# A transformer layer with expert look-up on one core: row norm taken out of the queries, head 0's queries first, queries made turned, scores read in PSUM

## The chip, the cores and the metric

One core of a Trainium2 chip. The time is device microseconds from start to end of one execution of the whole layer.

## The reference, cut to what matters

```
h = rms_norm(x, norm1_g);  x = x + mixer(h) @ w_out          # the front: products and attention
h = rms_norm(x, norm2_g)                                     # 256 rows of 2048
q = h @ w_query                                              # 2048 x 2048, 8 heads of 2 x 128
s = q . sub_keys                                             # per head two rows of 128 scores
top 16 of each, top 16 of the 256 sums -> expert_idx, g = softmax(best)
u, v = expert_u[expert_idx], expert_v[expert_idx]            # rows of 2048 floats
act = gelu(u . h);   x = x + sum (g * act) v
```

A row of h is x times a gain, times one factor for the row (rstd). This factor is a positive number common to all scores of a row, so the choice of the top 16 does not depend on it.

## The kernel before, in words

All 256 rows are two tiles (t) of 128 partitions. Products of fp32 are made of two halves: a weight step of 1024 columns (0.5 MB) is loaded by SP into one of four raw buffers, ACT copies it into `split_hi` (`hi_steps`, L450), DVE takes the difference into `split_lo` (`lo`, L653), and PE makes three products for each pair (`gemm_step`, L1165 to L1167). There are two split buffers, so step n needs the space of step n - 2; SP loads step n when lo n - 4 is done.

The front ends with the out-projection, 4 chunks of 512 columns with 8 steps each. After each chunk DVE adds it to x (`to_x1`, L967) and squares it. Then for the query product: the row norm is made (POOL takes the power, L375), ACT and DVE scale a tile of rows each (L475, L672), PE turns the rows (L1152), ACT and DVE split them into `ht` (L464, L681), and DVE multiplies the normed rows by the gain (L996) for the dots. `SK`, the keys, were turned during the out-projection (L1418, copied at L592).

The queries of chunk 0 (heads 0 and 1, both tiles) are made in eight steps, copied (`to_q`, L1005), turned by PE (L1431), copied by ACT (L577), multiplied with the keys (L1439) and the scores copied to `S` (`scores_out`, L1010). A head's selection has ten parts on DVE (`head_part`, L1025 to L1080); its last gives 16 row numbers for each partition, `pick_row`.

A loop of 276 picks follows, on each engine in its own order. There are 16 heads (8 for each tile) of 16 picks. At pick m POOL gathers 128 rows of u (1 MB) for pick m (L421), and 128 rows of v for pick m - 20 (L426), into a ring of 6 buffers; it needs the head's `pick_row` for the first. DVE takes the dot (L1084), does one part of the next head (k below 10), and adds half of the v row (L1102) for pick m - 20; PE adds the other half (L1449). Query chunks 1 to 3 stand in picks 0 to 7, 16 to 23 and 32 to 39, one step per pick: hi on ACT, and on DVE lo ahead of the pick's dot. No planner orders this: the order is the code's on each engine.

## Time and profile before

| | |
|---|---|
| median of 3 runs | 1861.89 us (1859.4 to 1862.16) |
| the profiled execution | 1861.74 us, span 1860.0 |
| DVE / PE / POOL / ACT busy | 72% / 69% / 44% / 20% |
| HBM read | 631.29 MB, 341 GB/s over the span |
| L1084, dots | 256, 2292 ns each |
| L1449, v rows on PE | 1024 products, 830 ns each |
| L653, lo | 152, 1223 ns each |
| granted clock of TensorE | 0.831 of full, mean |

Busy shares are means over the whole span; the stages have different limits, so the slices and stretches are read beside them. The chain is the work that ended last, followed back; it tells which engine or transfer a stretch waited for.

### The profile page before, as it was taken

Reading aid. Unit: us, or ns where it says so; the run is one execution under the profiler, and the core shown is the slowest. Engines: PE = TensorE matmul, PEld = TensorE weight load, DVE = VectorE, ACT = ScalarE, POOL = GpSimd, SP = SyncE. Lnnn points to the kernel's source line nnn. Section 1 sums busy time; section 2 is a strip of 40 time slices with the busy share of each in tenths; the row PEclk is TensorE's granted clock in tenths of the full one; section 3 lists DMA queues with packets and bytes.
Section 4 is the critical chain, followed back from the end, with each engine's and each line's share of the span. In section 5 each row is a group of like instructions: output and inputs, shape, how many; then the busy total and the mean of one; then the engine's idle time right before and its main releaser. Section 6 shows DMA issues by size and latency. Waiting matters only on the chain.

```text
span 1860.0 us, 12632 instructions
## 1 busy us (share of the span) xinstructions
PE 1284.4 (69%) x3739; PEld 691.6 (37%) x3739; DVE 1343.8 (72%) x1811; ACT 377.0 (20%) x642; POOL 821.0 (44%) x546
## 2 busy tenths in 40 slices
PE   7999999899755777555566555555655556555667
PEld 6888787778644444111121111111111111111122
DVE  5444555455669989878787877878788787877765
ACT  4333441534411212011110101011010101101001
POOL 1000000000034455666665656666566566656564
PEclk9999999889887989787866878787677787777779
DMA  7786545145359999999999999999999999999998
GB/s 214 209 207 191 156 137 158 47 159 183 113 202 415 414 418 420 422 422 415 422 422 422 422 417 409 422 422 421 422 412 417 421 418 422 417 416 422 415 423 358
DMA packets 128478, 634.38 MB, mean 341 GB/s; under 512 B 13426, under 2 KB 22212, under 8 KB 62372
## 3 DMA queue, kind: packets, MB, share of 16 engines
q0 software_dynamic: 74384, 538.74, 70.2%
q1 hardware_dynamic: 54036, 94.95, 16.6%
q8 instruction: 26, 0.43, 0.1%
q14 instruction: 32, 0.26, 0.0%
HBM read 631.29 MB, written 2.36 MB: 341 GB/s over the span
## 4 chain that ended last, share of the span: by engine, by line
DMA 40%; PE 33%; DVE 9%; POOL 8%; issue 7%; ACT 2%; POOLq 0%; SPq 0%; DVEq 0%; ACTq 0%
DMA big<-in_peer_expert_v,pick_row 23%; DMA big<-in_peer_expert_u,pick_row 16%; PE ps L1449 9%; POOL big L426 6%; PE ps L1165 6%; PE ps L1167 6%; PE ps L1166 6%; DVE big L1084 4%; POOL big L421 2%; DVE split_lo L653 1%; PE ps L1232 1%; DMA raw<-in_peer_w_query 1%; DVE ht L681 1%; PE ps L1152 1%; DMA big<-in_x 0%
## 5 line engine op out<-in xcount | busy, mean ns | idle before, releaser
L1449 PE MATMUL ps<-big,diag 128*128 128x512 f32 x1024 | 708.3, 830 | 486.1 <-DMA big<-in_peer_expert_v,pick_row 437.2
L1084 DVE CUSTOM_DVE_ANT_0 big<-big 128x2048 f32<-128x2048 f32 x256 | 586.4, 2292 | 210.4 <-DMA big<-in_peer_expert_u,pick_row 209.1
L426 POOL DMA_INDIRECT big<-in_peer_expert_v,pick_row x256 | 451.4, 1763 | 387.5 <-PE ps L1449 291.4
L1449 PEld LDWEIGHTS ps<-big,diag 128*128 128x128 f32 x1024 | 226.1, 243 | 957.1 <-DMA big<-in_peer_expert_v,pick_row 714.8
L421 POOL DMA_INDIRECT big<-in_peer_expert_u,pick_row x256 | 347.1, 1356 | 171.3 <-issue 71.6
L1102 DVE SCALAR_TENSOR_TENSOR big<-big,pick_w 128x1024 f32<-128x1024 f32 x256 | 327.4, 1279 | 46.8 <-DMA big<-in_peer_expert_v,pick_row 45.3
L653 DVE TENSOR_TENSOR split_lo<-raw,split_hi 128x1024 fp32r<-128x1024 f32 x152 | 185.8, 1223 | 169.7 <-ACT split_hi L450 139.4
L1165 PE MATMUL ps<-split_hi,ht 128*128 128x512 f32 x608 | 247.2, 407 | 48.4 <-DVE split_lo L653 48.4
L616 ACT ACTIVATE diag<-ident,pick_w 128x128 f32<-128x128 f32 x256 | 95.4, 395 | 803.0 <-PE ps L1449 489.2
L1166 PE MATMUL ps<-split_lo,ht 128*128 128x512 f32 x608 | 241.1, 397 | 0.0
L1167 PE MATMUL ps<-split_hi,ht 128*128 128x512 f32 x608 | 240.8, 396 | 0.0
L450 ACT ACTIVATE split_hi<-raw 128x1024 fp32r<-128x1024 f32 x130 | 137.5, 1060 | 240.3 <-PE ps L1167 224.4
L375 POOL TENSOR_TENSOR small<-small 128x2 f32<-128x2 f32 (+3 forms) x7 | 9.9, 1411 | 330.9 <-DVE small L734 137.5
L1165 PEld LDWEIGHTS ps<-split_hi,ht 128*128 128x128 f32 x608 | 116.3, 191 | 96.3 <-DVE split_lo L653 59.5
L1167 PEld LDWEIGHTS ps<-split_hi,ht 128*128 128x128 f32 x608 | 116.3, 191 | 25.9
L1166 PEld LDWEIGHTS ps<-split_lo,ht 128*128 128x128 f32 x608 | 116.4, 192 | 20.5 <-issue 0.5
L389 POOL DMA_DIRECT2D big<-bias_dram x8 | 4.3, 540 | 105.2 <-DVE split_lo L653 105.2
L607 ACT ACTIVATE pick_act<-pick_dot 128x16 f32<-128x16 f32 x16 | 3.4, 215 | 164.0 <-DVE pick_dot L1084 164.0
L681 DVE SCALAR_TENSOR_TENSOR ht<-ps,gain_cols,ht 128x256 fp32r<-128x256 f32 x48 | 19.8, 476 | 18.7 <-ACT ht L464 18.7
L497 ACT ACTIVATE split_hi<-raw 128x1024 fp32r<-128x1024 f32 x22 | 23.3, 1060 | 36.1 <-PE ps L1167 36.1
L1232 PE MATMUL ps<-raw,big 128*64 128x256 f32 x128 | 28.5, 381 | 0.1
L1152 PE MATMUL ps<-ident,big 128*128 128x128 f32 x96 | 16.0, 341 | 10.1 <-ACT big L475 10.1
(193 smaller groups left out, 699.4 us busy)
## 6 DMA issues: line engine op xcount, KB each, us to landing
raw<-in_w_in SPq DMA_DIRECT2D x88, 512.0 KB, 3.6
raw<-in_w_out SPq DMA_DIRECT2D x32, 512.0 KB, 4.3
raw<-in_peer_w_query SPq DMA_DIRECT2D x32, 512.0 KB, 11.2
raw<-in_cmp_k_w SPq DMA_DIRECT2D x8, 512.0 KB, 3.9
raw<-in_cmp_v_w SPq DMA_DIRECT2D x8, 512.0 KB, 4.2
big<-in_peer_expert_u,pick_row POOLq DMA_INDIRECT x256, 11.5
big<-in_peer_expert_v,pick_row POOLq DMA_INDIRECT x256, 11.4
big<-in_x SPq DMA_DIRECT2D x2, 1024.0 KB, 6.1
```

The source lines that it names most:

```text
L421: pool.indirect_dma_start(ring[g % RING], None, u_table, bass.IndirectOffsetOnAxis(pick_row[:, m:m + 1], 0)).then_inc(gathered[g % RING], 16)
L426: pool.indirect_dma_start(ring[g % RING], None, v_table, bass.IndirectOffsetOnAxis(pick_row[:, m - LAG:m - LAG + 1], 0)).then_inc(gathered ...
L450: act.activation(split_hi[:, s % SPLIT, :], raw[:, s % RAW, :], ACT.Copy).then_inc(hi_done, 1)
L616: act.activation(diag[:, m % DIAGS, :], ident[:, :], ACT.Copy, scale=pick_w[:, m:m + 1]).then_inc(sem("diag_made"), 1)
L653: dve.tensor_tensor(split_lo[:, slot % SPLIT, 0:width], raw[:, slot, 0:width], split_hi[:, slot % SPLIT, 0:width].bitcast(F32), ALU.subtra ...
L1084: dve.tensor_tensor_reduce(row, row, XN[:, m // (PICKS // TT), :], 1.0, 0.0, ALU.mult, ALU.add, pick_dot[:, m:m + 1]).then_inc(dotted, 1)
L1102: dve.scalar_tensor_tensor(out=v, in0=row[:, V_PE:D], scalar=pick_w[:, m:m + 1], in1=v, op0=ALU.mult, op1=ALU.add).then_inc(added, 1)
L1165: pe.matmul(acc[t], h_h, w_h, start=k == 0, stop=False)
L1166: pe.matmul(acc[t], h_h, w_l, start=False, stop=False)
L1167: ins = pe.matmul(acc[t], h_l, w_h, start=False, stop=k == KC - 1)
L1232: ins = pe.matmul(ps[0:64, 7, v * CMP_HIDDEN:(v + 1) * CMP_HIDDEN], BLK[:, v, l, :], raw[:, g % RAW, j * CMP_HIDDEN:(j + 1) * CMP_HIDDEN], ...
L1449: ins = pe.matmul(psf[:, t * V_PE + c:t * V_PE + c + 512], diag[:, m % DIAGS, :], row[:, c:c + 512], start=k == 0, stop=k == PICKS // TT - 1)
```

## The change

- The out-projection's loop (chunk c) also turns x of chunk c - 1 without its norm (`turn_x1`), splits it into `ht2`, and multiplies x by the gain into `XN` for the dots. The keys are turned in two halves of eight.
- The row factor is applied as the scale of the exponential and of the gelu on ACT.
- The first eight query steps are of another shape: four steps with all of k for head 0 (256 columns of the weight), then four for head 1. The weights are the stationary operand, so queries come out turned. One product moves both halves of the rows (512 columns), one moves the high half (256). `query_sum` adds the two halves out of PSUM.
- Step 4 and then head 0's scores follow step 3; steps 5 to 7 and head 1's scores come later. On DVE the second tile's sum and lo 6 and lo 7 stand behind head 0's selection.
- Chunks 1 to 3 are made of 24 products of 256 columns a step, with chunk 1 in picks 0 to 7, chunk 2 at every fourth pick from 16 to 44, and chunk 3 from 48 to 76.
- Scores are made for one head at a time and `head_part` reads them in PSUM. Head 1's parts begin at pick 4.
- Buffers move: four ring buffers take the place of `ht`, `ht2` that of the former four.

```diff
...
+HEAD_STEPS = STEPS_PER_CHUNK // 2
+HEAD_K = KC // HEAD_STEPS
...
+PART_AT = [4] + [0] * (HEADS - 1)
...
-        Q = part(TT * CHUNK, A_PROJ).rearrange("p (t n) -> p t n", t=TT)
-        PQT = part(4 * T).rearrange("p (w n) -> p w n", w=4)
+        PQT = part(HP * T, A_PROJ).rearrange("p (w n) -> p w n", w=HP)
         SK = part(2048).rearrange("p (w n) -> p w n", w=HP)
         SKT = part(2048).rearrange("p (w n) -> p w n", w=HP)
-        A_S = at_big[0]
-        S = part(4096).rearrange("p (t w n) -> p t w n", t=TT, w=HP)
-        gain_row2 = big[:, A_S:A_S + D]
+        gain_row2 = part(D)
         ring = [part(D) for _ in range(2)]
         assert at_big[0] <= A_XN
-        ring += [part(D, A_XN + TT * D + i * D) for i in range(RING - 2)]
+        ring += [more_rows[:, i, :] for i in range(RING - 2)]
+        ht2 = nc.alloc_sbuf_tensor_at("ht2", [P, KC, 2 * T], F32R, offset=at_sbuf["big"] + 4 * (A_XN + TT * D))
+        part(KC * 2 * T, A_XN + TT * D)
...
+            if use == 2:
+                return (4 + 2 * (k // 4 % 2)) * 512 + k % 4 * T
...
+        def score_at(head, s):
+            o = head % 2 * 2 * NKEYS + s * NKEYS
+            return ps[:, 6 + head % 4 // 2, o:o + NKEYS]
+        def query_step(m):
+            if m < STEPS_PER_CHUNK:
+                return 1, m
+            c, r = divmod(m - TOPK, 2 * TOPK)
+            if c in (0, 1) and r % 4 == 0:
+                return c + 2, r // 4
+            return None
+        QUERY_OUT = {9: 1, 46: 2, 78: 3}
...
-            with sp.Fori(0, W_CHUNKS) as c:
+            for n in range(STEPS_PER_CHUNK):
+                h, q = divmod(n, HEAD_STEPS)
+                sp.wait_ge(split_done, SP_QUERY + n - RAW + 1)
+                load(n % RAW, wq_k[:, HEAD_K * q:HEAD_K * (q + 1), h * 2 * HD:(h + 1) * 2 * HD], (HEAD_K, 2 * HD))
...
-                    if c == 2 and n == 2:
-                        act.wait_ge(sem("keys_turned"), 1)
-                        act.activation(SKT.rearrange("p w n -> p (w n)"), psf[:, 4 * 512:8 * 512], ACT.Copy).then_inc(sem("keys_ready"), 1)
                     hi_steps(c * 2 + RAW_OUT // RAW, c * STEPS_PER_CHUNK + SP_OUT, n, n + 1)
+                    if c < 3 and n == 3:
+                        act.wait_ge(sem("keys_turned"), c)
+                        b = 6 if c == 1 else 4
+                        act.activation(SKT[:, (c - 1) * NH:c * NH, :].rearrange("p w n -> p (w n)"), psf[:, b * 512:(b + 2) * 512],
+                                       ACT.Copy).then_inc(sem("keys_ready"), 1)
+                    if n == 5:
+                        turned_hi(2, G_NORM2, 4 * (c - 1), 4 * c)
             hi_steps(RAW_QUERY // RAW, SP_QUERY, 0, SPLIT)
-            scale_rows(7, X)
-            turned_hi(2, G_NORM2)
+            turned_hi(2, G_NORM2, 12, KC)
             hi_steps(RAW_QUERY // RAW, SP_QUERY, SPLIT, STEPS_PER_CHUNK)
-            queries_turned(0)
+            def query_out(c):
+                act.wait_ge(split_free, SP_QUERY + (c + 1) * STEPS_PER_CHUNK + 2)
+                act.activation(PQT[:, 4 * c:4 * c + 4, :].rearrange("p w n -> p (w n)"), psf[:, 4 * 512:6 * 512], ACT.Copy).then_inc(sem("pq_ready"), 1)
...
+                act.activation(v, v, ACT.Exp, scale=rstd[:, t:t + 1], accum_out=exp_sum[:, n:n + 1]).then_inc(sem("head_exp"), 1)
...
+                               ACT.Gelu_apprx_tanh, scale=rstd[:, t:t + 1]).then_inc(sem("head_acted"), 1)
...
+            act.wait_ge(sem("inverse_rms"), 7)
             head_exp(0)
             for m in range(STEPS):
                 n, k = divmod(m, TOPK)
-                if n + 1 < W_CHUNKS:
-                    c = n + 1
-                    if k < STEPS_PER_CHUNK:
-                        hi_steps(c * 2 + RAW_QUERY // RAW, c * STEPS_PER_CHUNK + SP_QUERY, k, k + 1)
-                    if k == 11:
-                        queries_turned(c)
+                if query_step(m):
+                    c, s = query_step(m)
+                    hi_steps(c * 2 + RAW_QUERY // RAW, c * STEPS_PER_CHUNK + SP_QUERY, s, s + 1)
+                if m in QUERY_OUT:
+                    query_out(QUERY_OUT[m])
...
-                                  XN[:, 0, t * CHUNK:(t + 1) * CHUNK])
+                                  MIX[:, t, 0:CHUNK])
...
+            def x1_gained(c):
+                for t in range(TT):
+                    v = slice(c * CHUNK, (c + 1) * CHUNK)
+                    dve.tensor_tensor(XN[:, t, v], X[:, t, v], gain_row2[:, v], ALU.mult).then_inc(sem("rows_gained"), 1)
...
-                    if s == 4 and c:
+                    if s == 3 and c:
                         x1_squares(c - 1)
-            for s in range(SPLIT):
-                lo(s, SP_QUERY + s)
+                    if s == 5 and c:
+                        turned_lo(2, G_NORM2, 4 * (c - 1), 4 * c)
+                    if s == 6 and c:
+                        dve.wait_ge(sem("gain_row_loaded"), 16)
+                        x1_gained(c - 1)
+            def query_sum(h, t):
+                dve.wait_ge(split_free, SP_QUERY + (h + 1) * HEAD_STEPS + 2)
+                v = slice(t * P, (t + 1) * P)
+                w = slice(T + t * P, T + (t + 1) * P)
+                dve.tensor_copy(PQT[:, 2 * h:2 * h + 2, v], ps[:, 2 * h:2 * h + 2, w]).then_inc(sem("pq_low"), 1)
+                dve.wait_ge(sem("pq_low"), 2 * h + t + 1)
+                dve.tensor_tensor(PQT[:, 2 * h:2 * h + 2, v], PQT[:, 2 * h:2 * h + 2, v], ps[:, 2 * h:2 * h + 2, v], ALU.add).then_inc(sem("pq_summed"), 1)
+            lo(0, SP_QUERY)
             to_x1(W_CHUNKS - 1)
+            lo(1, SP_QUERY + 1)
+            turned_lo(2, G_NORM2, 12, KC)
+            lo(2, SP_QUERY + 2)
+            lo(3, SP_QUERY + 3)
+            x1_gained(W_CHUNKS - 1)
             x1_squares(W_CHUNKS - 1)
+            lo(4 % RAW, SP_QUERY + 4)
             link(dve.tensor_reduce(ssq[:, 0:TT], x1_ssq.rearrange("p (t c) -> p t c", t=TT), AX_X, ALU.add))
-            inverse_rms(rstd[:, 0:TT], ssq[:, 0:TT], D)
...
-            turned_lo(2, G_NORM2)
-            dve.wait_ge(sem("gain_row_loaded"), 16)
-            for t in range(TT):
-                ins = dve.tensor_tensor(XN[:, t, :], XN[:, t, :], gain_row2, ALU.mult)
-            ins.then_inc(sem("rows_gained"), 1)
...
-                dve.wait_ge(split_free, SP_QUERY + (c + 1) * STEPS_PER_CHUNK + 2)
-                if c:
...
-                dve.tensor_copy(Q, ps[:, b:b + 2, :]).then_inc(acc_free, 1)
-            def scores_out(c):
...
-                dve.tensor_copy(S[:, :, 4 * c:4 * c + 4, :], ps[:, 6:8, :].rearrange("p t (w n) -> p t w n", n=NKEYS)).then_inc(sem("scores_read"), 1)
+            norms[0] += 1
+            dve.tensor_scalar(rstd[:, 0:TT], ssq[:, 0:TT], 1.0 / D, EPS, ALU.mult, ALU.add).then_inc(sem("mean_square"), 1)
+            query_sum(0, 0)
+            lo(5 % RAW, SP_QUERY + 5)
...
-                    dve.wait_ge(sem("scores_read"), h // 2 + 1)
+                    dve.wait_ge(sem("scores"), head + 1)
                     for s in range(2):
-                        done(dve.max(head_top[:, s, lo8], S[:, t, 2 * h + s, :]))
+                        done(dve.max(head_top[:, s, lo8], score_at(head, s)))
...
-            for s in range(SPLIT, STEPS_PER_CHUNK):
-                lo(s % RAW, SP_QUERY + s)
-            to_q(0)
-            scores_out(0)
             for part in range(10):
                 head_part(0, part)
-            dve.wait_ge(sem("rows_gained"), 1)
+            query_sum(0, 1)
+            for n in (6, 7):
+                lo(n % RAW, SP_QUERY + n)
+            dve.wait_ge(sem("rows_gained"), TT * W_CHUNKS)
             for m in range(STEPS):
                 n, k = divmod(m, TOPK)
-                if n + 1 < W_CHUNKS:
-                    c = n + 1
-                    if k < STEPS_PER_CHUNK:
-                        lo(k % RAW, SP_QUERY + c * STEPS_PER_CHUNK + k)
-                    if k == 9:
-                        to_q(c)
-                    if k == 14:
-                        scores_out(c)
+                if query_step(m):
+                    c, s = query_step(m)
+                    lo(s % RAW, SP_QUERY + c * STEPS_PER_CHUNK + s)
                 if m < PICKS:
                     pick_dot_of(m)
-                if n + 1 < HEADS and k < 10:
-                    head_part(n + 1, k)
+                if m == 1:
+                    query_sum(1, 0)
+                    query_sum(1, 1)
+                if n + 1 < HEADS and 0 <= k - PART_AT[n] < 10:
+                    head_part(n + 1, k - PART_AT[n])
                 if m >= LAG:
                     if (m - LAG) % TOPK == 0:
...
+            def turn_keys(half):
+                b = 4 if half else 6
+                for w in range(NH):
+                    ins = pe.transpose(psf[:, b * 512 + w * P:b * 512 + (w + 1) * P], SK[:, half * NH + w, :], ident[:, :])
+                ins.then_inc(sem("keys_turned"), 1)
...
+            def turn_x1(c):
+                pe.wait_ge(sem("x1_ready"), c + 1)
+                for k in range(4 * c, 4 * c + 4):
+                    for t in range(TT):
+                        o = turned_at(2, k) + t * P
+                        ins = pe.transpose(psf[:, o:o + P], X[:, t, k * P:(k + 1) * P], ident[:, :])
+                    if k % 2:
+                        ins.then_inc(sem("rows_turned"), 1)
...
-                if c == 2:
-                    pe.wait_ge(sem("keys_loaded"), 16)
-                    for w in range(HP):
-                        ins = pe.transpose(psf[:, 4 * 512 + w * P:4 * 512 + (w + 1) * P], SK[:, w, :], ident[:, :])
-                    ins.then_inc(sem("keys_turned"), 1)
-                gemm_chunk(CH_OUT + c, (CH_OUT + c) % 2, c * STEPS_PER_CHUNK + SP_OUT, 1)
-            pe.wait_ge(sem("keys_ready"), 1)
-            turn_rows(2, 8)
...
-                if c:
-                    pe.wait_ge(sem("scores_read"), c)
-                for w in range(4):
...
-                ins.then_inc(sem("pq_turned"), 1)
...
-                pe.wait_ge(sem("pq_ready"), c + 1)
-                for t in range(TT):
...
+                for n in range(STEPS_PER_CHUNK):
+                    if n == 2 and c == 1:
+                        pe.wait_ge(sem("keys_loaded"), 16)
+                        turn_keys(0)
+                    if n == 2 and c == 2:
+                        pe.wait_ge(sem("ht_lo"), 2 * KC + 4)
+                        turn_keys(1)
+                    if n == 4:
+                        if c > 1:
+                            pe.wait_ge(sem("keys_ready"), c - 1)
+                        turn_x1(c - 1)
+                    gemm_step(acc, n % SPLIT, (2 * n, 2 * n + 1), CHUNK, SP_OUT + c * STEPS_PER_CHUNK + n)
...
+            def first_queries(n):
+                h, q = divmod(n, HEAD_STEPS)
+                pe.wait_ge(split_done, SP_QUERY + n + 1)
+                for j in range(HEAD_K):
+                    k = HEAD_K * q + j
+                    for w in range(2):
+                        o = j * 2 * HD + w * HD
+                        w_h = split_hi[:, n % SPLIT, o:o + HD]
+                        w_l = split_lo[:, n % SPLIT, o:o + HD]
+                        if k < KC - 1:
+                            pe.matmul(ps[:, 2 * h + w, :], w_h, ht2[:, k, :], start=k == 0, stop=False)
+                            ins = pe.matmul(ps[:, 2 * h + w, 0:T], w_l, ht2[:, k, 0:T], start=False, stop=False)
+                        else:
+                            pe.matmul(ps[:, 2 * h + w, 0:T], w_l, ht2[:, k, 0:T], start=False, stop=False)
+                            ins = pe.matmul(ps[:, 2 * h + w, :], w_h, ht2[:, k, :], start=False, stop=True)
+                ins.then_inc(split_free, 1)
...
+            def queries(c, n):
+                pe.wait_ge(split_done, SP_QUERY + c * STEPS_PER_CHUNK + n + 1)
+                if n == 0 and c > 1:
+                    pe.wait_ge(sem("pq_ready"), c - 1)
+                for j in range(2):
+                    k = 2 * n + j
                     for w in range(4):
-                        ins = pe.matmul(ps[:, 6 + t, w * P:(w + 1) * P], PQT[:, w, t * P:(t + 1) * P], SKT[:, 4 * c + w, :],
-                                        start=True, stop=True)
+                        o = j * CHUNK + w * HD
+                        w_h = split_hi[:, n % SPLIT, o:o + HD]
+                        w_l = split_lo[:, n % SPLIT, o:o + HD]
+                        acc = ps[:, 4 + w // 2, w % 2 * T:(w % 2 + 1) * T]
+                        pe.matmul(acc, w_h, ht2[:, k, 0:T], start=k == 0 and w % 2 == 0, stop=False, skip_group_check=True)
+                        pe.matmul(acc, w_l, ht2[:, k, 0:T], start=False, stop=False, skip_group_check=True)
+                        ins = pe.matmul(acc, w_h, ht2[:, k, T:2 * T], start=False, stop=k == KC - 1, skip_group_check=True)
+                ins.then_inc(split_free, 1)
+            def head_scores(head):
+                t, h = divmod(head, NH)
+                if head >= 4:
+                    pe.wait_ge(head_step, (head - 4) * HEAD_OPS + 6)
+                if h >= 2:
+                    pe.wait_ge(sem("pq_ready"), h // 2)
+                for s in range(2):
+                    ins = pe.matmul(score_at(head, s), PQT[:, 2 * h + s, t * P:(t + 1) * P], SKT[:, 2 * h + s, :], start=True, stop=True)
                 ins.then_inc(sem("scores"), 1)
...
-            gemm_chunk(CH_QUERY, CH_QUERY % 2, SP_QUERY, 2)
-            turn_chunk(0)
-            chunk_scores(0)
+            pe.wait_ge(sem("keys_ready"), 2)
+            pe.wait_ge(acc_free, CH_QUERY + 1)
+            pe.wait_ge(sem("ht_lo"), 2 * KC + 8)
+            for n in range(HEAD_STEPS - 1):
+                pe.wait_ge(sem("ht_lo"), 2 * KC + HEAD_K * (n + 1))
+                first_queries(n)
+                if n == 0:
+                    turn_x1(W_CHUNKS - 1)
+            pe.wait_ge(sem("ht_lo"), 3 * KC)
+            pe.wait_ge(acc_free, CH_QUERY + 2)
+            first_queries(HEAD_STEPS - 1)
+            first_queries(HEAD_STEPS)
+            pe.wait_ge(sem("pq_summed"), 1)
+            head_scores(0)
+            for n in range(HEAD_STEPS + 1, STEPS_PER_CHUNK):
+                first_queries(n)
+            pe.wait_ge(sem("pq_summed"), 4)
+            head_scores(1)
             for m in range(STEPS):
                 n, k = divmod(m, TOPK)
-                if n + 1 < W_CHUNKS:
-                    c = n + 1
-                    if k < STEPS_PER_CHUNK:
-                        gemm_step([ps[:, 4 + t, :] for t in range(TT)], k % SPLIT, (2 * k, 2 * k + 1), CHUNK,
-                                  SP_QUERY + c * STEPS_PER_CHUNK + k)
-                    if k == 10:
-                        turn_chunk(c)
-                    if k == 12:
-                        chunk_scores(c)
+                if query_step(m):
+                    queries(*query_step(m))
+                if k == TOPK - 1 and n + 2 < HEADS:
+                    head_scores(n + 2)
                 if m >= LAG:
                     pick_add(m - LAG)
```

## Rows read from the trace of the kernel before

**Rows 1.** Page, the span in 40 equal slices.
```profile
DMA  7786545145359999999999999999999999999998
GB/s 214 209 207 191 156 137 158 47 159 183 113 202 415 414 418 420 422 422 415 422 422 422 422 417 409 422 422 421 422 412 417 421 418 422 417 416 422 415 423 358
```

**Rows 2.** Page, DMA queue: packets, MB, share of 16 engines.
```profile
q0 software_dynamic: 74384, 538.74, 70.2%
```

**Rows 3.** Stretches: PE, PEld, DVE, ACT, POOL busy, PEclk, DMA share, GB/s.
```profile
537.00:545.00 8.00, 5.21 (x12) 3.80 (x12) 3.51 (x4) 2.21 (x4) 6.78 (x5) 0.54 0.76 257
545.00:553.00 8.00, 5.60 (x17) 3.95 (x18) 7.12 (x17) 1.95 (x2) 7.09 (x4) 0.79 1.01 407
...
561.00:569.00 8.00, 5.61 (x23) 3.99 (x23) 7.97 (x15) 1.06 (x1) 1.97 (x2) 1.00 1.02 414
...
1840.00:1850.00 10.00, 8.00 (x18) 2.75 (x17) 5.21 (x5) 1.21 (x3) 2.74 (x2) 1.00 1.01 418
```

**Rows 4.** Chain of waits, 434 to 537: start us, us, what.
```profile
434.06 1.75 PE ps L1418 x16
...
479.77 0.24 PE ps L1167
...
482.41 1.14 DVE big L967
...
490.39 6.64 DVE ht L681 x16
497.03 4.40 DVE big L996 x2
...
521.17 1.24 DVE big L1005
...
524.65 2.06 PE ps L1439 x16
...
528.00 0.50 DVE big L1025 x2
...
536.99 1.10 POOL big L421
```

**Rows 5.** Timeline of DVE and ACT in the out-projection: start, us, operation [idle before].
```profile
424.28 1.23 DVE L653 TENSOR_TENSOR split_lo<-raw,split_hi 128x1024 fp32r<-128x1024 f32 x1 [0.29 <-ACT split_hi L450]
427.03 1.23 DVE L653 TENSOR_TENSOR split_lo<-raw,split_hi 128x1024 fp32r<-128x1024 f32 x1 [1.52 <-ACT split_hi L450]
...
469.09 1.06 ACT L450 ACTIVATE split_hi<-raw 128x1024 fp32r<-128x1024 f32 x1 [1.68 <-PE ps L1167]
```

**Rows 6.** Line L1290: duration ns min/median/max, first and last start.
```profile
L1290 PE MATMUL ps<-ht,split_hi x16: 276/278/281, 286.8 to 292.0; 128*24 128x256 f32 x16
```

**Rows 7.** Groups of instructions: busy us, mean ns | idle before.
```profile
L1108 DVE TENSOR_TENSOR big<-big,ps 128x1024 f32<-128x1024 f32 x2 | 2.4, 1218 | 0.8 <-PE ps L1449 0.8
...
L1165 PEld LDWEIGHTS ps<-split_hi,ht 128*128 128x128 f32 x608 | 116.3, 191 | 96.3 <-DVE split_lo L653 59.5
```

**Rows 8.** Timeline of PE, the first step beside the gathers.
```profile
539.53 0.79 PE L1165 MATMUL ps<-split_hi,ht 128*128 128x512 f32 x1 [12.82 <-DVE split_lo L653]
...
544.35 0.39 PE L1167 MATMUL ps<-split_hi,ht 128*128 128x512 f32 x1
```

**Rows 9.** Timeline of DVE, picks 2, 3 and the end of head 1's selection.
```profile
551.82 2.29 DVE L1084 CUSTOM_DVE_ANT_0 big<-big 128x2048 f32<-128x2048 f32 x1
...
554.43 1.21 DVE L653 TENSOR_TENSOR split_lo<-raw,split_hi 128x1024 fp32r<-128x1024 f32 x1
555.55 2.29 DVE L1084 CUSTOM_DVE_ANT_0 big<-big 128x2048 f32<-128x2048 f32 x1
...
582.97 0.17 DVE L1080 TENSOR_TENSOR pick_row<-big 128x16 uint32<-128x16 f32 x1
```

**Rows 10.** Timeline of POOL, gather 16, the first of head 1.
```profile
586.13 2.25 POOL L421 DMA_INDIRECT big<-in_peer_expert_u,pick_row  x1 [2.58 <-DVE pick_dot L1084]
```

**Rows 11.** Line L421, 530 to 640: gathers of u, from issue to landing.
```profile
DMA to landing us min/median/max: 5.7/11.6/16.9
```

More of the change, by code:

```diff
@@ L274, in turned_at, with turned @@
         def turned_at(use, k):
+            if use == 2:
+                return (4 + 2 * (k // 4 % 2)) * 512 + k % 4 * T
             return (2 * KC // 4 + k % 4) * T if use == 1 and k < KC // 2 else k * T
+        def turned(use):
+            return ht2 if use == 2 else ht
+        def score_at(head, s):
[9 more added lines that the diff above has]
+        QUERY_OUT = {9: 1, 46: 2, 78: 3}
         def loaded(eng, slot, g):
@@ L463, in turned_hi @@
                     o = turned_at(use, k)
-                    act.activation(ht[:, k, 0:T], psf[:, o:o + T], ACT.Copy,
+                    act.activation(turned(use)[:, k, 0:T], psf[:, o:o + T], ACT.Copy,
                                    scale=gain_cols[:, gain0 + k:gain0 + k + 1]).then_inc(sem("ht_hi"), 1)
@@ L680, in turned_lo @@
                         dve.wait_ge(sem("ht_hi"), KC * use + k + 2)
-                    dve.scalar_tensor_tensor(out=ht[:, k, T:2 * T], in0=psf[:, o:o + T],
+                    dve.scalar_tensor_tensor(out=turned(use)[:, k, T:2 * T], in0=psf[:, o:o + T],
                                              scalar=gain_cols[:, gain0 + k:gain0 + k + 1],
-                                             in1=ht[:, k, 0:T].bitcast(F32), op0=ALU.mult,
+                                             in1=turned(use)[:, k, 0:T].bitcast(F32), op0=ALU.mult,
                                              op1=ALU.subtract).then_inc(sem("ht_lo"), 1)
```

31 lines of the change are left out of this document (10 added, 21 removed).

## The prediction

> **What bounds the kernel now.** I read the busy slices of the page first: from the thirteenth slice to the last the DMA engines are 9 tenths or more busy and move 415 to 422 GB/s; before that they move half or less [rows 1]. The kernel has two parts, a front of products and then a stream of expert rows, 538.74 MB on POOL's queue [rows 2]. The stretches say how sharp the border is: 257 GB/s in the first 8 us after 537, 407 in the next 8, 418 at 1840 [rows 3]. So from about 540 on the end is set by bytes, and the front matters only through the moment of the first gather. The chain around it [rows 4] shows what stands ahead: PE's last out-projection product ends at 480.0, the first gather is issued at 536.99, 57.0 us later. Between lie the last adds and squares, the row norm, turning and splitting (490.4 to 497.0), the gain (4.4 us), eight query steps, a copy, a turn, a copy, scores, a copy, and head 0's selection, 528.0 to 536.7. The change works on these 57 us. Anything afterwards matters only if the DMA queues run dry.
>
> **Out-projection, parts added.** A step takes 1.06 + 1.68 = 2.74 us, paced by PE [rows 5]. Of the 32 transposes of the rows, 24 move in here; 16 take 1.75 us [rows 4], 0.109 each, so 24 x 0.109 = **+2.6 us**, all on the path. The keys' 16 are only divided in two. DVE gets four 0.42 us splits per chunk (6.64 / 16 [rows 4]) and two products with the gain, 4.40 / 8 = 0.55 each. It idles 1.5 us between two lo steps, and squares of 1.3 us fitted into one such hole, leaving 0.29 [rows 5]. The splits (1.7 us) are a little larger than a hole, but PE is 0.9 us longer at work there; the gain's 1.1 us fits. ACT's four copies (1.5 us) fit in its 1.68 plus 0.9. Cost of these nothing; were the cover gone, about 1 us in each of three chunks. The out-projection ends at 480.0 + 2.6 = 482.6. I call this T.
>
> **From T to the first gather, in us after T.** The loads of query steps 0 to 3 went out during the out-projection.
> - PE: query step 0 at once (k 0 to 3 are already turned). It has 8 products of 512 columns at 0.23 (2.74 / 12) and 8 of 256 columns. The trace has 48 products of 256 columns; the first of each group of three start from 286.8 to 292.0, so 5.2 / 45 = 0.115 us apart [rows 6]. Step: 8 x 0.23 + 8 x 0.115 = 2.8, as before.
> - Meanwhile DVE adds chunk 3 (1.14 and its semaphore [rows 4]), then lo 1 until 2.7. PE turns k 12 to 15 at 2.8 to 3.7, then step 1 until 6.6. ACT copies them until 5.0 and makes hi 2 until 6.1; DVE splits until 6.0, lo 2 until 7.4. PE waits 0.8 us, step 2 until 10.2.
> - lo 3 is done at 9.0, step 3 ends at 13.0. The sum of the two halves out of PSUM (256 columns each, about 0.42 like the split, and semaphores) ends at 14.1. Ahead of it DVE has gained, squared and done lo 4, until 13.0: just hidden.
> - PE stands in step 4 until 15.8, two score products end at 16.2. lo 5 (15.4) is hidden behind them. Head 0's selection took 8.7 us [rows 4] and starts now: 25.0, plus 0.3 for POOL: **25.3**.
> First gather at 482.6 + 25.3 = 507.9, **29.1 us earlier**. The norm, its scaling, the gain, three copies of 1.0 to 1.2 and the turn of the queries are gone from this path, and four of eight query steps stand behind it.
>
> The selection now reads scores in PSUM. Rows: a 1024-wide DVE operation with a PSUM source took 1218 ns [rows 7], one from SBUF 1.23 us [rows 5]; no price, and I take none. The Trainium skill (VectorE: DVE Perf Modes, The TRN2 errata) speaks against this part: a fixed 120 cycles for a PSUM source against 58. By it the six PSUM reads ahead of the first gather would cost an estimated 6 x 62 / 0.96 GHz = 0.4 us; the trace does not agree.
>
> **Bytes moved behind the first gather.** Before, 12 query loads were out by 537, 20 after it; now lo 5 has released load 9, so 22 come after: 2 x 0.524 MB / 0.42 = **+2.5 us**.
>
> **Does the stream stay full?** It has 6 buffers, and only gathers of u until pick 20. Again after T:
> - Gathers 0 to 5 go out at 25 to 35. DVE sums the second tile (0.9) and does lo 6 and lo 7 until 28.2. PE idled from 16, and after such a pause a step ran from 539.53 at the low clock of 1.2 GHz, its last product at 544.4 [rows 8], some 5.2 us: step 6 ends at 32.4. Pick 0 needs lo 8, which needs hi 8, which needs step 6: lo 8 ends at 34.7, dot 0 at 36.9, lo 9 and dot 1 at 40.2, query sums at 42.0.
> - PE waits for these sums before it makes head 1's scores and step 8, again on the low clock: 42.4 to 47.6. hi 10, then lo 10 at 50.0. **DVE stands 6.7 us.** Queued behind it are dot 2 and with it gather 8, and every later pick.
> - Then, by lo 1.13 and dot 2.2 as they follow each other in 551.8 to 555.6 [rows 9], and selection parts only from pick 4 on: dot 2 52.2, dot 3 55.5, dot 5 62.6, dot 7 70.7, dot 9 76.2, dot 13 88.9, head 1's rows at **89.7**, that is 64.4 us after the first gather. Before it was 582.97 + 0.2 - 536.99 = 46.2 [rows 4, 9].
> - The engines have until then 16 rows (2.5 us each) and 10 query loads (1.25 each), 52.5 us of work, from 28.3 on: dry at 80.8. Gather 16 may go at 89.9 and flows 3 us later. **Gap: about 12 us**, less what late loads fill: I take 11. Before, gather 16 was never late: POOL waited 2.6 us for DVE's dot, not for the rows [rows 10].
> After that two gathers go with each pick, 5 us of transfer against some 4.5 us of DVE work, and a query step only at every fourth: full, as before.
>
> **Sum** against the profiled execution, 1861.7 (span 1860.0; the median of the runs is 1861.9, the same): 1861.7 - 29.1 + 2.5 + 11 = **1846**. The bounds: nothing lost in the gap, and DVE waits hidden by the ring; or every one of the 0.4 to 1 us waits of this count somewhat longer, 3 us before the gather, and a gap of 17. That makes 1835 to 1855. About 0.2% is what a measurement can tell from no change (3.7 us).
>
> **Rivals.**
> 1. *The stream never runs dry.* For: before, DVE was busy 7.97 of 8 us at picks 5 and 6 and the engines stayed full [rows 3]; landings took 11.6 us in the median [rows 11], so a queue is there. Against: it empties by the count above. 1861.7 - 29.1 + 2.5 = 1835. Chance 0.18.
> 2. *The gap is larger.* Waits at picks 2 to 7 for loads that stand behind gathers, up to 16.9 us each [rows 11], hold DVE in order. Load 14 leaves at 50.0 and hi 14 is wanted at 64: slack of some 14 us, so about 3 us are lost for each of three loads at the longest landing: gap 20, 1855. Chance 0.14.
> 3. *Short products do not cover their weight load*, and the result is slower. The change has 16 loads in a step instead of 12, and 24 in the steps of chunks 1 to 3. A load takes 191 ns [rows 7]. Exposed, a head step takes 2.8 + 16 x 0.19 = 5.8; five stand ahead of the first gather: +14 after slack. A step at picks 0 to 7 takes 24 x (0.115 + 0.19) = 7.3 against DVE's 3.9 to 4.4 per pick: +3.2 x 7 = 22 on head 1. 1846 + 14 + 22 = 1882. With x us exposed per load the loss is about (5 x 16 + 6 x 24) x = 224 x: it decides from x = 0.07. Against it: scores with a load of 128 columns each went 16 in 2.06 us, 0.13 apiece, load included [rows 4], so at most 0.02 is exposed. Chance 0.04. The Trainium skill (TensorE: Matmul & The Clock Gate, LDWEIGHTS and its perf modes) says that a load overlaps a running matmul only where the row groups differ; here both use all rows, and by that rule this rival would be the outcome. The trace speaks against the rule.
> 4. *The added work does not fit the out-projection and the front gains little*: each chunk's splits delay the next lo, and the sum waits for DVE's squares. For a result within 0.2% it would have to eat 12 us of 29, against holes of 1.5 us per step. Chance 0.04.
>
> **Numbers.** The forecast (1846, 1838 to 1852 in itself) has 0.6. Of both signs only the third rival is slower; with an unseen wait in the front I give slower 0.05, within 0.2% 0.05, faster 0.90. The range 1835 to 1857 leaves out less than 2 in 10.
>
> **What would show it.** The chain: last out-projection product at 482.6, query step 0 right behind it, head 0's first maximum near 499, first gather near 508. The timeline: query products of 256 columns 0.115 apart at the high clock; a DVE wait of about 7 us before lo 10; head 1's rows 64 us after the first gather. The stretches: GB/s full from 516 to about 563, a dip of about 11 us before 575, then 420 until the end, and no other dip. Wrong would be: no dip; a first gather later than 515; DVE waiting for query weights; or a stream under 410 GB/s after pick 20.

## The result, and the profile after

The changed kernel takes 1845.9 us in the median (1844.2 to 1847.9, 4 runs) against 1860.9 for the kernel before on the same chip: ratio 0.992, 95% interval 0.9903 to 0.9937. The forecast was 1846 in a range of 1835 to 1857. The profiled execution of the changed kernel took 1844.2, span 1842.5.

The slices of the page show a dip that was not there before [rows 1], in the thirteenth slice, right behind the start of the stream:

```profile
DMA  7776544155497999999999999999999999999998
GB/s 216 209 209 194 160 137 160 47 172 174 156 400 312 419 420 420 418 420 422 421 422 419 422 406 423 421 420 413 420 406 423 422 417 422 415 403 418 422 422 354
```

The stretches place it (columns as in [rows 3]): full until 556, then 162 and 80 GB/s, 388 from 572 on and 423 from 580 on.

```profile
548.00:556.00 8.00, 0.98 (x7) 0.59 (x5) 7.97 (x13) 1.02 (x1) 2.59 (x3) 0.83 1.03 416
556.00:564.00 8.00, 0.00 (x0) 0.00 (x0) 7.93 (x16) 0.00 (x0) 0.00 (x0) 0.50 0.39 162
564.00:572.00 8.00, 0.07 (x1) 0.07 (x1) 7.84 (x9) 3.86 (x6) 4.81 (x3) 0.50 0.24 80
572.00:580.00 8.00, 5.39 (x24) 5.12 (x24) 5.97 (x14) 0.03 (x1) 6.78 (x5) 0.67 1.00 388
580.00:588.00 8.00, 0.82 (x4) 0.82 (x5) 7.53 (x12) 0.00 (x0) 7.03 (x4) 0.54 1.01 423
```

POOL's timeline shows both ends of the first head, gather 0 and gather 16. Gather 16 had waited 12.5 us for head 1's row numbers; before, it waited for a dot [rows 10].

```profile
501.97 1.10 POOL L451 DMA_INDIRECT big<-in_peer_expert_u,pick_row  x1 [11.60 <-DVE pick_row L1119]
...
566.58 2.74 POOL L451 DMA_INDIRECT more_rows<-in_peer_expert_u,pick_row  x1 [12.53 <-DVE pick_row L1119]
```

The chain from the out-projection to the first gather (it answers to [rows 4]) has lost the norm, the gain and the copies. The last out-projection product starts at 476.27, the last score product ends at 492.9, and the selection follows:

```profile
476.27 0.23 PE ps L1203
476.50 0.28 PE ps L1492
...
479.83 0.85 ACT ht L494 x2
480.70 1.66 DVE ht L712 x4
482.38 1.24 DVE split_lo L684
483.62 0.14 issue
483.76 0.47 PE ps L1492
...
492.46 0.46 PE ps L1523 x4
492.94 0.51 DVE big L1064 x2
```

DVE's timeline shows its two stands (waits in which it does nothing), before lo 8 and before lo 10; the wait is in the brackets:

```profile
510.67 1.23 DVE L684 TENSOR_TENSOR split_lo<-raw,split_hi 128x1024 fp32r<-128x1024 f32 x1 [5.93 <-ACT split_hi L480]
...
525.40 1.23 DVE L684 TENSOR_TENSOR split_lo<-raw,split_hi 128x1024 fp32r<-128x1024 f32 x1 [6.37 <-ACT split_hi L480]
```

**A correction for the start.** The attention ahead of the out-projection is not touched by the change, but the first ACT step of the out-projection's weights behind the attention stands at 388.28 in the profile before and at 382.32 after. So I read three marks in every profile, which do not depend on it: first gather minus that ACT step, gather 16 minus first gather, and end of the span minus first gather. All are in the table below. The wait for the first gather and for gather 16 together give the date of gather 16.

### The profile page after: what moved, and what is told of

It reads as the page before. It is cut to its first block, busy times and chain, and to the rows that moved or that the text cites. A ratio compares the mean times of both kernels' runs of the same rounds, so it can differ in the third digit from the quotient of the medians.

```text
span 1842.5 us, 13182 instructions
## 1 busy us (share of the span) xinstructions
PE 1281.6 (70%) x4027; PEld 706.7 (38%) x4027; DVE 1337.1 (73%) x1816; ACT 376.0 (20%) x641; POOL 823.6 (45%) x546
## 4 chain that ended last, share of the span: by engine, by line
DMA 44%; PE 34%; DVE 8%; issue 6%; POOL 6%; ACT 2%; POOLq 0%; SPq 0%; DVEq 0%; ACTq 0%
DMA more_rows<-in_peer_expert_v,pick_row 20%; DMA big<-in_peer_expert_v,pick_row 12%; PE ps L1532 11%; DMA more_rows<-in_peer_expert_u,pick_row 8%; PE ps L1201 6%; PE ps L1203 6%; PE ps L1202 6%; POOL more_rows L456 3%; DMA big<-in_peer_expert_u,pick_row 3%; DVE more_rows L1123 2%; POOL big L456 2%; DVE split_lo L684 1%; POOL more_rows L451 1%; PE ps L1268 1%; DVE big L1123 1%
## 5 line engine op out<-in xcount | busy, mean ns | idle before, releaser
L1532 PE MATMUL ps<-more_rows,diag 128*128 128x512 f32 x680 | 479.9, 845 | 319.1 <-DMA more_rows<-in_peer_expert_v,pick_row 296.2
L1123 DVE CUSTOM_DVE_ANT_0 more_rows<-more_rows,big 128x2048 f32<-128x2048 f32 x170 | 389.5, 2291 | 146.4 <-DMA more_rows<-in_peer_expert_u,pick_row 145.6
L456 POOL DMA_INDIRECT more_rows<-in_peer_expert_v,pick_row x170 | 295.2, 1736 | 263.6 <-PE ps L1532 197.4
L1532 PE MATMUL ps<-big,diag 128*128 128x512 f32 x344 | 236.9, 827 | 157.9 <-DMA big<-in_peer_expert_v,pick_row 145.3
L451 POOL DMA_INDIRECT more_rows<-in_peer_expert_u,pick_row x170 | 232.9, 1370 | 90.9 <-issue 50.1
L1123 DVE CUSTOM_DVE_ANT_0 big<-big 128x2048 f32<-128x2048 f32 x86 | 197.0, 2291 | 68.7 <-DMA big<-in_peer_expert_u,pick_row 68.1
L1141 DVE SCALAR_TENSOR_TENSOR big<-more_rows,pick_w,big 128x1024 f32<-128x1024 f32 x170 | 217.4, 1279 | 31.0 <-DMA more_rows<-in_peer_expert_v,pick_row 29.8
L456 POOL DMA_INDIRECT big<-in_peer_expert_v,pick_row x86 | 156.2, 1816 | 128.7 <-PE ps L1532 94.7
L451 POOL DMA_INDIRECT big<-in_peer_expert_u,pick_row x86 | 116.9, 1359 | 51.2 <-issue 24.1
L1141 DVE SCALAR_TENSOR_TENSOR big<-big,pick_w 128x1024 f32<-128x1024 f32 x86 | 110.0, 1279 | 20.0 <-DMA big<-in_peer_expert_v,pick_row 19.4
```

Of the source, the lines that this page charges most:

```text
L451: pool.indirect_dma_start(ring[g % RING], None, u_table, bass.IndirectOffsetOnAxis(pick_row[:, m:m + 1], 0)).then_inc(gathered[g % RING], 16)
L456: pool.indirect_dma_start(ring[g % RING], None, v_table, bass.IndirectOffsetOnAxis(pick_row[:, m - LAG:m - LAG + 1], 0)).then_inc(gathered ...
L1123: dve.tensor_tensor_reduce(row, row, XN[:, m // (PICKS // TT), :], 1.0, 0.0, ALU.mult, ALU.add, pick_dot[:, m:m + 1]).then_inc(dotted, 1)
L1141: dve.scalar_tensor_tensor(out=v, in0=row[:, V_PE:D], scalar=pick_w[:, m:m + 1], in1=v, op0=ALU.mult, op1=ALU.add).then_inc(added, 1)
L1532: ins = pe.matmul(psf[:, t * V_PE + c:t * V_PE + c + 512], diag[:, m % DIAGS, :], row[:, c:c + 512], start=k == 0, stop=k == PICKS // TT - 1)
```

## The experiments

| kernel | first ACT step | to first gather | gather 0 to 16 | gather 0 to end | median us | ratio to before (interval) |
|---|---|---|---|---|---|---|
| before | 388.3 | 148.7 | 49.1 | 1323.0 | 1860.9 | |
| ctl_before | 381.7 | 148.6 | 48.9 | 1325.2 | 1862.1 | 1.0008 (0.9998 to 1.0018) |
| changed | 382.3 | 119.65 | 64.6 | 1340.5 | 1845.9 | 0.992 (0.9903 to 0.9937) |
| ctl_after | 385.0 | 119.6 | 64.7 | 1338.5 | 1846.4 | 0.9924 (0.9907 to 0.994) |
| part6 | 384.0 | 119.65 | 69.1 | 1344.0 | 1848.9 | 0.9932 (0.9915 to 0.9948) |
| part2 | 388.3 | 119.7 | 60.7 | 1335.4 | 1844.9 | 0.9908 (0.9885 to 0.9931) |
| q8_early | 387.8 | 119.7 | 65.1 | 1339.3 | 1845.6 | 0.9913 (0.9896 to 0.9929) |
| all8 | 383.2 | 128.25 | 62.4 | 1337.5 | 1854.3 | 0.997 (0.9958 to 0.9983) |
| turn_late | 386.2 | 122.9 | 64.0 | 1339.3 | 1849.4 | 0.9936 (0.9918 to 0.9954) |
| close | 382.2 | 119.8 | 64.6 | 1339.3 | 1844.5 | 0.9926 (0.9909 to 0.9943) |
| fill | 385.75 | 121.7 | 47.7 | 1324.5 | 1834.65 | 0.9865 (0.9845 to 0.9886) |
| fill_again | 380.7 | 121.7 | 48.1 | 1325.8 | 1834.7 | 0.9874 (0.9857 to 0.989) |
| fill_part4 | 384.8 | 121.7 | 57.8 | 1332.8 | 1841.4 | 0.9911 (0.9894 to 0.9928) |
| fill_s0 | 386.5 | 121.2 | 48.3 | 1324.2 | 1831.9 | 0.9852 (0.9834 to 0.9869) |

Each row's marks come from one profile. close and the last three rows were timed on another chip than the rest: there the kernel before gave 1857.9 in the median, beside the other experiments 1860.4 and 1861.1. Between the two groups the ratio is compared, not the median.

### The two controls

No edit.

> The kernel before, unchanged, as a control. In the profile of the changed kernel the unchanged code between about 350 and 388 us took 6.0 us less than in that of the kernel before (the first ACT step of the out-projection after the attention at 382.3 against 388.3), with a granted clock of 0.87 against 0.69 there. Theory A: this is chance between executions of any kernel (where TensorE's clock falls and rises); then this step starts anywhere between 381 and 389 in either kernel, and the time stays at 1861 within 2. Theory B: it belongs to the change; then it starts again at 388 here, within 0.5.

> The changed kernel, unchanged, as a control. Theory A (chance of the clock): the first ACT step of the out-projection starts between 381 and 389, not tied to 382.3; first gather 119.6 us after it, head 1's row numbers 64.2 us after the first gather, time 1846 within 2. Theory B (part of the change): 382.3 within 0.5.

The ACT step, in the control of the kernel before and then in that of the changed one:

```profile
381.72 1.06 ACT L450 ACTIVATE split_hi<-raw 128x1024 fp32r<-128x1024 f32 x1 [8.51 <-PE ps L1167]
```

```profile
384.97 1.06 ACT L480 ACTIVATE split_hi<-raw 128x1024 fp32r<-128x1024 f32 x1 [9.70 <-PE ps L1203]
```

Theory A holds: the same kernel gave 388.3 and 381.7, and over all profiles the step lies anywhere from 380.7 to 388.3 whatever the edit. The granted clock in the stretch 358 to 388 goes with it: 0.60 where the step came last (388.3, the kernel before), 0.72 at 385.0 (ctl_after), 0.83 at 381.7 and 382.3 (ctl_before and the changed kernel), 0.89 at 380.7 (fill_again). This scatter of some 7 us also lies in the times: the kernel before gave 1855.2 to 1863.7 in 13 runs. The marks scatter by 0.1 us (to the first gather) and 2 us (to the end).

### Head 1's selection two dots later, and two dots earlier

```diff
-PART_AT = [4] + [0] * (HEADS - 1)
+PART_AT = [6] + [0] * (HEADS - 1)     # part6;  [2] in part2
```

> Head 1's selection begins at pick 6 instead of pick 4, so its row numbers come two dots later. Theory (the stream runs dry until head 1's row numbers are there, and each us they are late is lost): two dots of 2.2 us later, nothing else moved; row numbers 68.6 us after the first gather instead of 64.2, time 1846 + 4.4 = 1850. Rival (the dip belongs to slow dots and to query loads, not to the row numbers): no change within 1.

> Head 1's selection begins at pick 2 instead of pick 4; nothing else. Theory (the dry stretch ends with head 1's row numbers, set by DVE's dots ahead of them): two dots less, 4.4 us; but at picks 2 to 11 eight of the dots now carry a lo too, so the selection's last part stands behind the same query steps: row numbers 59.8 us after the first gather (64.2 in the changed kernel, 68.6 with pick 6), the time from first gather to end 1335 (1339.5 in the changed kernel, 1344.0 with pick 6). Rival (the stream's total is bound by something later): row numbers earlier, the end the same within 1.

The three kernels are a scale: gather 16 comes 60.7, 64.6 and 69.1 us after the first, and the end 1335.4, 1339.5 (mean of two) and 1344.0. Over 8.4 us the end moved 8.6: by the marks, while there is a dip, each us by which head 1's row numbers come later is about a us of time. The medians (1844.9, 1846.1, 1848.9) move the same way but only by 3.9 us; the start scatters by enough to hide the rest, but that it did so here is not shown.

The whole table bears the marks out. From gather 16 to the end ("gather 0 to end" less "gather 0 to 16") it took 1273.8 to 1277.7 us in all fourteen profiles, with a dip and without. The change brought gather 16 from 197.8 us behind the ACT step (148.7 + 49.1) to 184.3, 13.5 us earlier, and the end came 13.6 us earlier by the marks.

### Query step 8 ahead of head 1's scores

```diff
-            pe.wait_ge(sem("pq_summed"), 4)
-            head_scores(1)
             for m in range(STEPS):
                 n, k = divmod(m, TOPK)
                 if query_step(m):
                     queries(*query_step(m))
+                if m == 1:
+                    pe.wait_ge(sem("pq_summed"), 4)
+                    head_scores(1)
```

> PE makes query steps 8 and 9 before head 1's scores, so it no longer waits for DVE's query sums ahead of step 8. Theory: DVE's stand of 6.4 us before lo 10 goes, the clock is still high for step 8, head 1's row numbers come 6.4 us earlier (57.8 after the first gather), the dry stretch is shorter by the same, time 1846 - 6.4 = 1839.5. Rival (the gathers are behind the wait anyway; the ring covers it): the stand goes, time the same within 1. Second rival: the stand is only moved to a later lo, since the loads of steps 10 to 13 land late behind the gathers; then 2 to 3 us are gained.

The stand before lo 10 went, and nothing was gained: gather 16 came at 65.1. The second rival named the reason, though no 2 to 3 us were left over either. DVE now stood at four later lo steps, 7.2 us in sum against the 6.4 that went:

```profile
533.11 1.23 DVE L684 TENSOR_TENSOR split_lo<-raw,split_hi 128x1024 fp32r<-128x1024 f32 x1 [2.51 <-ACT split_hi L480]
539.12 1.23 DVE L684 TENSOR_TENSOR split_lo<-raw,split_hi 128x1024 fp32r<-128x1024 f32 x1 [2.17 <-ACT split_hi L480]
545.15 1.23 DVE L684 TENSOR_TENSOR split_lo<-raw,split_hi 128x1024 fp32r<-128x1024 f32 x1 [1.53 <-ACT split_hi L480]
550.01 1.23 DVE L684 TENSOR_TENSOR split_lo<-raw,split_hi 128x1024 fp32r<-128x1024 f32 x1 [1.02 <-ACT split_hi L480]
```

ACT, which makes the hi half for them, waited for the loads. Its timeline of this run, hi 11 to 14:

```profile
526.06 1.07 ACT L480 ACTIVATE split_hi<-raw 128x1024 fp32r<-128x1024 f32 x1 [4.97 <-DMA raw<-in_peer_w_query]
532.02 1.06 ACT L480 ACTIVATE split_hi<-raw 128x1024 fp32r<-128x1024 f32 x1 [4.90 <-DMA raw<-in_peer_w_query]
538.03 1.06 ACT L480 ACTIVATE split_hi<-raw 128x1024 fp32r<-128x1024 f32 x1 [4.95 <-DMA raw<-in_peer_w_query]
544.07 1.06 ACT L480 ACTIVATE split_hi<-raw 128x1024 fp32r<-128x1024 f32 x1 [4.97 <-DMA raw<-in_peer_w_query]
```

Here query loads land 6.0 us apart while gathers are queued, and DVE, which takes lo ahead of each dot, waits for them. In the changed kernel ACT's steps hi 10 to 15 all waited for PE. The stand on PE and the late loads are two bounds of nearly the same height; one hid the other.

### All eight query steps ahead of head 0

```diff
-            for part in range(10):
-                head_part(0, part)
             query_sum(0, 1)
             for n in (6, 7):
                 lo(n % RAW, SP_QUERY + n)
+            for part in range(10):
+                head_part(0, part)
...
+            for n in range(HEAD_STEPS + 1, STEPS_PER_CHUNK):
+                first_queries(n)
             pe.wait_ge(sem("pq_summed"), 1)
             head_scores(0)
-            for n in range(HEAD_STEPS + 1, STEPS_PER_CHUNK):
-                first_queries(n)
```

> Undoes 'head 0 first': all eight steps of the first query chunk before head 0's scores, the rest as changed. Theory (two ends count: the first gather, and head 1's row numbers): the first gather 8.4 us later, since three steps of 2.8 stand ahead of the scores; DVE's stand before lo 8 (5.9) is gone, so head 1's row numbers come 60 us after the first gather instead of 64.2; the end 8.4 - 4 = +4 us, 1850.5. Rival (only the first gather counts): +8.4, 1855. Second rival (only head 1's row numbers count, the first three steps come for nothing): the same within 1.

The first gather is 8.6 us later (128.25 against 119.65), the rest 2.0 shorter: +6.6 by the marks, +8 in the medians. "Head 0 first" is worth 6 to 8 us of the whole. I had expected 4 us back and a time of 1850.5; the median of 1854.3 lies nearer to the rival by which only the first gather counts (1855). The marks still speak for two dates, for gather 16 came 2.3 us sooner behind the first, and the end with it. A new wait took part of the expected 4 us, since the first dot now stood for the row itself:

```profile
517.14 2.29 DVE L1123 CUSTOM_DVE_ANT_0 big<-big 128x2048 f32<-128x2048 f32 x1 [3.09 <-DMA big<-in_peer_expert_u,pick_row]
```

### The rows turned after the out-projection

```diff
                     if n == 4:
-                        if c > 1:
-                            pe.wait_ge(sem("keys_ready"), c - 1)
-                        turn_x1(c - 1)
...
+            turn_x1(0)
+            turn_x1(1)
+            pe.wait_ge(sem("ht_lo"), 2 * KC + 4)
+            turn_x1(2)
             pe.wait_ge(sem("ht_lo"), 2 * KC + 8)
+            turn_x1(3)
...
-                if n == 0:
-                    turn_x1(W_CHUNKS - 1)
```

ACT and DVE split k 0 to 15 behind the out-projection as well; the product with the gain stays in it.

> Undoes 'rows turned beside the out-projection': all sixteen k are turned and split after it, the gain stays where the change put it. Theory by its steps: the out-projection ends 2.6 us earlier (24 transposes of 0.109), but the split of k 12 to 15 on ACT then ends at 9 to 10 us after it, hi 2 and lo 2 about 5 us later than in the changed kernel; the first gather is 2.7 us later than there, counted from the start of the out-projection (122.3 against 119.6), and the time +2.7. Rival: most of the 29 us came from this part (four fifths of the turning is off the path), and it costs 6 us or more to undo.

+3.2 us to the first gather (122.9), +3 in the median. Turning beside the out-projection is worth no more than that, for the 24 transposes lengthen the out-projection itself by 2.5 us (see the next section). Of the 29 us, "head 0 first" is 8.6 and this part 3.2. Some 17 us are left by subtraction, if the parts simply add, for the norm and its scaling, the gain, the copies and the turn of the queries. These I did not take back one at a time, so their shares are not shown.

### Query chunks 2 and 3 close together

```diff
-QUERY_OUT = {9: 1, 46: 2, 78: 3}
+QUERY_OUT = {9: 1, 25: 2, 41: 3}
```

`query_step` gives the steps of chunks 2 and 3 to picks 16 to 23 and 32 to 39.

> The changed kernel with query chunks 2 and 3 put back into eight picks each (16 to 23, 32 to 39) instead of every fourth pick. Theory (beside u and v gathers DVE has slack at every pick, so it does not matter where the steps stand): time 1846 within 1.5, first gather to end 1339.5 within 1.5. Rival (at picks 16 to 19 the stream refills after its dry stretch and only u gathers go: an added 1.2 us of lo per pick holds it): 2 to 4 us longer, GB/s under 415 in the stretches behind the dip.

No difference (1339.3 to the end, against 1339.5): it did not matter which of these picks the steps stand in.

### lo 6 and lo 7 inside head 0's selection, head 1's from pick 0

```diff
             for part in range(10):
                 head_part(0, part)
+                if part == 2:
+                    lo(6 % RAW, SP_QUERY + 6)
+                if part == 6:
+                    lo(7 % RAW, SP_QUERY + 7)
             query_sum(0, 1)
-            for n in (6, 7):
-                lo(n % RAW, SP_QUERY + n)
+            query_sum(1, 0)
+            query_sum(1, 1)
...
-                if m == 1:
-                    query_sum(1, 0)
-                    query_sum(1, 1)
...
-PART_AT = [4] + [0] * (HEADS - 1)
+PART_AT = [0] + [0] * (HEADS - 1)
```

> lo 6 and lo 7 go into head 0's selection, all query sums stand right behind it, head 1's selection begins at pick 0. Theory: the first gather comes 2.4 us later (two lo steps of 1.2); query steps 6 and 7 are done while DVE selects, loads 10 and 11 land ahead of the gathers, DVE's two stands (5.9 and 6.4 us) and the four empty picks go; head 1's row numbers 46 to 50 us after the first gather, as in the kernel before, no dry stretch; from first gather to end 1325; time 1846.4 + 2.4 - 14 = 1835. Rival (late query loads pace the picks whatever the order, as the run with step 8 early showed them to): stands come back at lo 12 to 15, row numbers at 55 or later, time 1842 or more.

> The kernel with lo 6 and lo 7 inside head 0's selection and head 1's selection from pick 0, once more, beside its variants: 1835 within 2, first gather 121.7 us after the out-projection's first ACT step, first gather to end 1324.5 within 1.5, whatever the clock does in the attention.

1834.65 and 1834.7, against 1835 forecast: the first gather 2.1 us later, 14 us less behind it. Gather 16 of the second of these runs waits for a dot again, as in the kernel before, and where the dip was the stream is full (411 to 420 GB/s in every stretch of 8 us from 516 to 588):

```profile
550.45 2.24 POOL L451 DMA_INDIRECT more_rows<-in_peer_expert_u,pick_row  x1 [2.58 <-DVE pick_dot L1123]
```

```profile
548.00:556.00 8.00, 0.00 (x0) 0.00 (x0) 8.00 (x7) 2.13 (x2) 4.94 (x3) 0.50 1.03 414
556.00:564.00 8.00, 1.90 (x9) 1.90 (x10) 7.92 (x8) 1.25 (x2) 7.09 (x4) 0.50 1.01 417
```

> The kernel with lo 6 and lo 7 inside head 0's selection, but head 1's selection beginning at pick 4 as in the change. Separates its two ingredients. Theory (work of the DMA engines until gather 16: 16 rows of 2.5 us and now 8 to 10 query loads of 1.25 us, dry some 53 to 55 us after the first gather): row numbers four dots later than in that kernel, 44.5 + 8.8 = 53.4 us after the first gather, dry for 1 to 4 us; first gather to end 1327 (1324.5 there). Rival (the empty picks were the whole loss, the stands came for nothing): 1324.5 + 8.8 = 1333.

With the four empty picks put back (`PART_AT = [4] + ...`), gather 16 comes at 57.8 instead of the 53.4 of my count, and the end is 7.7 us later than in these kernels (1332.8 against the mean of 1325.1). The theory's mechanism held, its size did not: it dated the row numbers by dots alone. DVE stood again for late loads (1.5 and 2.2 us before two lo steps), and the dip was longer than the 1 to 4 us of the theory: 247, 197 and 385 GB/s in the three stretches of 8 us from 556 on are an estimated 8 us of transfer short of 418. The rival's number (1333) came out right, but its reason is only part of it, for these stands are there too. Set against the changed kernel, this run says what the lo steps and sums alone gave back: 6.7 us behind the first gather (1339.5 - 1332.8). The start at pick 0 gave the other 7.7; without the moved lo steps it was not tried.

> As that kernel, but head 0's scores stand ahead of query step 4, and lo 5 also goes into the selection. Theory: scores 1.7 us earlier (14.5 after the out-projection instead of 16.2), lo 5 no longer hidden, 1.2: first gather 0.5 us earlier (121.2 against 121.7), time 1834.5. Rival (PE, which now waits for DVE's sum before step 4, drops to its low clock and steps 4 to 7 take 5.2 us each): the first gather 0.5 us earlier, but lo 7 and lo 8 wait and the time is 3 us longer.

```diff
             first_queries(HEAD_STEPS - 1)
-            first_queries(HEAD_STEPS)
             pe.wait_ge(sem("pq_summed"), 1)
             head_scores(0)
+            first_queries(HEAD_STEPS)
```

lo 5 goes behind part 1 of the selection, lo 6 and lo 7 behind parts 4 and 7. The first gather came 0.5 us earlier, as counted, at 121.2. The time was not 3 us longer, so the rival is out. The median of 1831.9 is the lowest of the study, 12.6 us below close on the same chip, whose marks are those of the changed kernel; whether it beats the kernel without this last edit by more than 0.5 us is within the scatter.

## Why the prediction was right, point by point

- **What bounds it**: right. From 600 to 1800 us the stream moved 407 to 422 GB/s in every 100 us of every kernel, and only the dates of the first gather and of gather 16 moved the end.
- **Out-projection**: forecast +2.6, measured 94.2 us from the first ACT step to the end of the last product (476.5 - 382.3) against 91.7 (480.0 - 388.3): +2.5. Behind a chunk's splits and behind its product with the gain, DVE still waited 0.8 and 0.3 us for ACT, so its added work was covered.
- **From there to the first gather**: forecast 25.3, measured 501.97 - 476.5 = 25.5. The 256-column products started 0.12 apart, the selection took 501.67 - 492.94 = 8.73 us with scores in PSUM against 8.70 before, so there was no price for PSUM, as the rows had it. The Trainium skill (VectorE: DVE Perf Modes, The TRN2 errata) would have made it an estimated 0.4 us longer; the trace shows 0.03.
- **Sum of the front**: forecast 29.1 us earlier; 148.7 - 119.65 = 29.05.
- **Pick 0 to head 1's row numbers**: forecast stands of 5.3 (33.5 - 28.2) and 6.7 us, measured 5.93 and 6.37; row numbers 64.4 us after the first gather forecast, 566.14 + 0.18 - 501.97 = 64.35 measured.
- **The gap**: forecast 11 us and 2.5 for the loads that moved, 13.5 together. Measured, by the means of two profiles each, 1339.5 - 1324.1 = 15.4, 1.9 us more, which is no more than this mark scatters by. The stretches tell the dip itself apart: 162, 80 and 388 GB/s from 556 to 580 are an estimated 11.9 us of transfer short of 418. So 12 was the better figure than the 11 that I took, and no late loads had to be struck off.
- **What was read wrongly**: the step named DVE's stand before lo 10 as what makes the picks late. Its size was right, its role was not: with the stand removed nothing was gained (gather 16 at 65.1 against 64.6), since query loads behind gathers then set the same date. The second rival had this mechanism; it decides only once the stand is gone.
- **The rivals**: the stream did run dry; the dip was not 20 us; short products covered their weight loads. On this the trace of the changed kernel is plain:

```profile
L1493 PEld LDWEIGHTS ps<-ht,split_lo x60: 187/188/338, 476.4 to 510.7; 128*128 128x128 f32 x60
L1493 PE MATMUL ps<-ht,split_lo x60: 279/281/416, 476.6 to 511.0; 128*128 128x256 f32 x60
```

A load took 188 ns, and in chunk 1 products with a new load each follow 0.11 us apart (523.93, 524.04, 524.16 us): they overlap, though every load and product uses all rows. The Trainium skill (TensorE: Matmul & The Clock Gate, The mechanism) says that a load overlaps products in flight "only when row_grp differs"; that sentence does not hold here. The same section also lets a load into a background weight buffer go ahead of them, which would fit; no run here shows which it was.
- **What was luck**: that the terms add up to the median so closely. By the marks the change is worth 29.05 - 15.4 = 13.65 us, not the forecast 15.6, and 1861.7 less that is 1848. The medians say 15.0, and the start alone scatters by 7 us between executions.

## What to carry to other kernels

When a front feeds a stream that is bound by bytes, two dates count: when the first transfer goes, and when the second batch of addresses is ready, compared with how long the first batch keeps the engines busy. Work taken off the path to the first date is given back in part if it is put ahead of the second: here 29.05 us were won and 15.4 given back, a forecast 2.5 of them as the bytes of loads that moved. Small steps that feed another engine can go inside a long serial chain: here two of them cost 2.1 us ahead of the first gather and gave back 6.7 behind it. With them in place, the second head's selection could begin four picks sooner, which gave another 7.7.

## What the runs showed of the hardware that I had not expected

- Loads of 0.5 MB from SP's queue landed in 3.5 us in the median during the out-projection, before any gather (changed kernel, 400 to 476). Beside POOL's gathers the median was 10.7 us in the changed kernel, 15.3 in q8_early and 18.0 in fill_again. In the last two, ACT waited for loads that landed 6.0 us apart, an estimated 87 GB/s of the 412 to 415 that the core moved in those stretches of q8_early. The rows: the changed kernel, 400 to 476 and 502 to 560; q8_early, 507 to 560; fill_again, 502 to 560:

```profile
raw<-in_peer_w_query SPq DMA_DIRECT2D x4, 512.0 KB, 3.5
raw<-in_peer_w_query SPq DMA_DIRECT2D x10, 512.0 KB, 10.7
raw<-in_peer_w_query SPq DMA_DIRECT2D x10, 512.0 KB, 15.3
raw<-in_peer_w_query SPq DMA_DIRECT2D x8, 512.0 KB, 18.0
```

- Unchanged code took up to 7.6 us more or less from one execution to the next (380.7 to 388.3). It went with how long TensorE's clock stood at 1.2 GHz ahead of 388 us (granted 0.60 to 0.89 over the stretch from 358); what makes it stand there longer in one execution stays open. Marks behind it tell more than the time: the one to the first gather scattered by 0.1 us, the one to the end by 2.
